# Four norms at stage borders, taken by token halves, in a two-block transformer kernel

## The chip, the cores and the metric

The kernel runs on one core of one Trainium2 chip. The metric is the device time of one execution, in microseconds; the number given for a kernel is the median of its runs. The core's engines are TensorE (PE, with its weight loads as PEld), VectorE (DVE), ScalarE (ACT), GpSimd (POOL) and SyncE (SP), which here issues the loads. They work side by side and meet at semaphores.

## What is computed

Two blocks of a network over 256 latent tokens of width 1024, in float32. The first block is an attention and recurrence layer and a neighbourhood attention layer. The second block carries 256 further context tokens beside the latent ones, so 512 in all. Its layers are feed-forward ("ffn"), a short convolution, and grouped-query attention. All of them have this frame:

```
mod = silu(c) @ mod_w[i] + mod_b[i]                       # shift, scale, gate; one set for latents, one for context
h   = rms(x) * g * (1 + scale) + shift                    # the norm in front of each layer
x   = x + 0.5 * gate * ((silu(h @ w1) * (h @ w3)) @ w2)    # feed-forward
x   = x + gate * ((b * dwconv3(c * v)) @ w_out)           # convolution: b, c, v = split(h @ w_in)
x   = x + gate * (attend(q, k, v) @ w_o)                  # attention; keys and values from latents and context
```

where `rms(x) = x / sqrt(mean(x*x) + 1e-6)` runs over the 1024 features of a token. A norm therefore needs every feature of a token, which is every output tile of the stage in front of it.

## The kernel before

Activations lie with features on the 128 partitions: `XT` is 128 x 8 x 512, eight k of 128 features, with the latent tokens in columns 0 to 255 and the context tokens in 256 to 511. The matmuls work in float32 by two parts: activation = `Hh` + `Hl`, weight = `Wh` + `Wl`, and `three` (line 1296) issues three matmuls for each product. Each weight tile of 128 x 2048 (128 x 1408 in the second half of a feed-forward) is loaded by SyncE into `raw`, copied by ScalarE into `Wh` (`split`, line 513), and the remainder `Wl` is made by VectorE (`split`, line 799). Two buffers each hold raw, Wh and Wl, so ScalarE's copy of tile n waits for TensorE to end tile n - 2 (`tile_done`), and TensorE's tile n waits for `lo_ready`.

The stages run in a fixed order (`STAGES`), each tile of 256 output features (`conv_in` 12 tiles, `conv_out` 4, `ffn*_up` 22). In `ffn*_down` an output of 128 features takes two tiles, one for each half of the contraction, 16 tiles in all. The sixth entry of a stage is `gemv`: so many rows of the modulation weights are dotted on VectorE with each tile (`modulation_of`, line 848; two `dot` instructions of 128 x 1024 for each row set, one for latents and one for context).

A stage that feeds a norm adds its output to `XT` (`residual` on VectorE, line 903, and `ffn_down`, line 938). ScalarE squares each finished k (`splits`, line 560), GpSimd adds the squares up in `tmp[:, 2]` (line 459), and TensorE sums over partitions by matmuls with ones into `psN` (`sum_of_sums`, then the last one or two k in `norm`). VectorE makes the mean, GpSimd the power -0.5, TensorE spreads it over partitions (`spread`, line 1350), and then VectorE (`scaled`), ScalarE (`Hh`) and VectorE (`Hl`) make the eight k of the next input; the first tile of the next stage waits for each k (`h_ready`). Every one of these steps takes all 512 tokens. The copies of the second weight tile of the next stage stand between the mean and the scaling:

```python
split(S[name].n0 + 1, early=True)
dve.wait_ge(n_spread, i + 1)
```

`SUMMED` says how many of GpSimd's additions are made (6 behind a feed-forward, 5 behind `conv_out`). The order of each engine is written out by hand at the end of its program (`norm`, `linear`, `ffn_down` in turn).

## Time and profile before

| | us |
|---|---|
| median of 3 runs | 2092.98 |
| lowest and highest | 2090.76, 2093.58 |
| the profiled execution | 2093.39 |
| its span on the core | 2091.6 |
| TensorE busy | 1908.9 (91%) |
| TensorE weight loads busy | 1624.7 (78%) |
| VectorE busy | 1402.9 (67%) |
| ScalarE busy | 683.9 (33%) |
| GpSimd busy | 126.5 (6%) |

The profile is one execution. A row of its timeline gives the start from the beginning of the span, the duration, the engine, the line of the kernel, what is written and read, and in brackets how long the engine was idle before and what released it. A matmul's duration overlaps the next; the distance of two starts is what one costs. PEclk is the granted clock of TensorE as a share of 2.4 GHz; its two levels are 1.00 (2.4 GHz) and 0.50 (1.2 GHz).

### The profile page before, as it was taken

The numbers are of one execution on the slowest core, as the hardware profiler recorded it, in microseconds if no ns is written. First come the engines' busy times: TensorE is split into PE (matmuls) and PEld (weight loads), VectorE is DVE, ScalarE is ACT, GpSimd is POOL, SyncE is SP. The second block draws the span as 40 slices with busy tenths as digits, with TensorE's granted clock in tenths as the row PEclk, the third lists the DMA queues.
The fourth block names the chain that finished last, engine by engine and source line by source line (L and its number), as shares of the span: only waits on it lengthen the run. The fifth ranks groups of instructions, "written<-read, shape, count | busy, mean of one in ns | idle before, by whom it ended". The sixth has DMA issues, their size and how long they took to land.

```text
span 2091.6 us, 26725 instructions
## 1 busy us (share of the span) xinstructions
PE 1908.9 (91%) x10092; PEld 1624.7 (78%) x10092; DVE 1402.9 (67%) x2091; ACT 683.9 (33%) x910; POOL 126.5 (6%) x78
## 2 busy tenths in 40 slices
PE   2973799789999998998999999989999998889998
PEld 2952788778888887886788888878888887678998
DVE  7868799986666676668766666676666225856554
ACT  2443356432222213332322222232222223444432
POOL 2001300200000010002000001100000010010000
PEclk9975799889999999999999999999999999999999
DMA  9840955423443443334333344434333323223444
GB/s 377 313 168 3 238 206 188 181 93 149 150 150 125 167 175 124 134 148 151 121 143 133 146 149 159 164 121 151 141 134 118 105 94 122 91 81 141 162 163 158
DMA packets 75737, 315.77 MB, mean 151 GB/s; under 512 B 19060, under 2 KB 22904, under 8 KB 56344
## 3 DMA queue, kind: packets, MB, share of 16 engines
q1 hardware_dynamic: 75136, 314.15, 41.9%
q8 instruction: 36, 0.59, 0.1%
q10 hardware_dynamic: 536, 0.79, 0.1%
q14 instruction: 29, 0.24, 0.0%
HBM read 313.86 MB, written 1.06 MB: 151 GB/s over the span
## 4 chain that ended last, share of the span: by engine, by line
PE 74%; DVE 18%; ACT 3%; issue 2%; DMA 1%; POOL 1%; SPq 0%; DVEq 0%; ACTq 0%
PE acc L1294 72%; DVE Wl L810 4%; ACT Wh L526 2%; DVE tmp L797 2%; PE psN L1294 1%; DVE psGT L842 1%; DVE psGT L839 1%; DVE psGT L845 1%; DVE najunk L845 1%; DVE najunk L842 1%; DVE XT L797 1%; DMA afirst<-in_ada_w 1%; DVE small L967 1%; PE psN L1356 1%; DVE tmp L985 1%
## 5 line engine op out<-in xcount | busy, mean ns | idle before, releaser
L1294 PE MATMUL acc<-Hh,Wh 128*128 128x512 f32 (+1 forms) x2320 | 809.0, 349 | 57.1 <-DVE Hl L797 23.4
L1294 PE MATMUL acc<-Hl,Wh 128*128 128x512 f32 (+1 forms) x2320 | 801.1, 345 | 0.0
L1294 PE MATMUL acc<-Hh,Wl 128*128 128x512 f32 (+1 forms) x2320 | 800.4, 345 | 0.0
L810 DVE TENSOR_TENSOR Wl<-raw,Wh 128x2048 fp32r<-128x2048 f32 (+1 forms) x214 | 449.6, 2101 | 273.0 <-ACT Wh L526 273.0
L1294 PEld LDWEIGHTS acc<-Hh,Wh 128*128 128x128 f32 x2320 | 448.5, 193 | 119.3 <-issue 62.2
L526 ACT ACTIVATE Wh<-raw 128x2048 fp32r<-128x2048 f32 (+1 forms) x214 | 374.3, 1749 | 352.0 <-PE acc L1294 336.7
L1294 PEld LDWEIGHTS acc<-Hl,Wh 128*128 128x128 f32 x2320 | 448.7, 193 | 50.6 <-issue 0.7
L1294 PEld LDWEIGHTS acc<-Hh,Wl 128*128 128x128 f32 x2320 | 448.1, 193 | 50.7
L1294 PE MATMUL acc<-hidh,Wh 128*128 128x512 f32 (+1 forms) x704 | 259.0, 368 | 0.9 <-DVE Wl L810 0.9
L1294 PE MATMUL acc<-hidl,Wh 128*128 128x512 f32 (+1 forms) x704 | 258.6, 367 | 0.0
L1294 PE MATMUL acc<-hidh,Wl 128*128 128x512 f32 (+1 forms) x704 | 258.6, 367 | 0.0
L797 DVE SCALAR_TENSOR_TENSOR tmp<-tmp,acc 128x512 f32<-128x512 f32 (+1 forms) x176 | 109.3, 621 | 130.0 <-ACT tmp L593 120.3
L593 ACT ACTIVATE tmp<-acc 128x512 f32<-128x512 f32 (+1 forms) x88 | 47.9, 544 | 453.2 <-PE acc L1294 453.2
L842 DVE SCALAR_TENSOR_TENSOR psGT<-graw,cb 128x1024 f32<-128x1024 f32 x122 | 169.3, 1388 | 0.4
L459 POOL TENSOR_TENSOR tmp<-tmp 128x512 f32<-128x512 f32 (+1 forms) x44 | 89.8, 2041 | 1313.7 <-ACT tmp L557 1156.4
L845 DVE SCALAR_TENSOR_TENSOR psGT<-graw,cb 128x1024 f32<-128x1024 f32 x122 | 154.0, 1262 | 4.2
L1294 PEld LDWEIGHTS acc<-hidh,Wh 128*128 128x128 f32 x704 | 132.6, 188 | 24.6 <-DVE Wl L810 1.1
L1294 PEld LDWEIGHTS acc<-hidh,Wl 128*128 128x128 f32 x704 | 132.6, 188 | 23.9
L1294 PEld LDWEIGHTS acc<-hidl,Wh 128*128 128x128 f32 x704 | 132.6, 188 | 23.8
L934 DVE TENSOR_TENSOR hidl<-tmp,hidh 128x512 f32 (+3 forms) x88 | 55.1, 626 | 71.5 <-ACT hidh L596 71.5
L797 DVE SCALAR_TENSOR_TENSOR XT<-acc,mod,XT 128x256 f32 (+3 forms) x88 | 36.0, 454 | 88.3 <-PE acc L1294 88.3
L596 ACT ACTIVATE hidh<-tmp 128x512 f32 (+3 forms) x88 | 50.9, 578 | 133.8 <-DVE tmp L797 133.8
(222 smaller groups left out, 1193.8 us busy)
## 6 DMA issues: line engine op xcount, KB each, us to landing
raw<-in_ffn_up SPq DMA_DIRECT2D x88, 1024.0 KB, 4.7
graw<-in_mod_w SPq DMA_DIRECT2D x144, 512.0 KB, 5.4
raw<-in_ffn_down SPq DMA_DIRECT2D x64, 704.0 KB, 4.0
graw<-in_ada_w SPq DMA_DIRECT2D x32, 512.0 KB, 6.2
raw<-in_odd_in SPq DMA_DIRECT2D x16, 1024.0 KB, 4.9
raw<-in_even_in SPq DMA_DIRECT2D x12, 1024.0 KB, 6.8
raw<-in_conv_in SPq DMA_DIRECT2D x12, 1024.0 KB, 4.7
afirst<-in_ada_w SPq DMA_DIRECT2D x8, 1024.0 KB, 13.1
```

Source lines behind the costliest of these rows:

```text
L459: nc.gpsimd.tensor_tensor(tmp[:, 2, 0:n], tmp[:, 0 if k == 1 else 2, 0:n], tmp[:, k % 2, 0:n], ALU.add).then_inc(n_sum, 1)
L526: nc.scalar.activation(Wh[:, half, 0:f], raw[:, slot, 0:f], ACT.Copy).then_inc(hi_ready, 1)
L593: nc.scalar.activation(tmp[:, b, 0:s.tokens], acc[b][0][:, 0:s.tokens], ACT.Tanh, scale=0.5)\
L596: nc.scalar.activation(at3(hidh, t, s.tokens), tmp[:, 3, 0:s.tokens], ACT.Copy).then_inc(ffn_hi, 1)
L797: return nc.vector.scalar_tensor_tensor(out=out, in0=a, scalar=s, in1=b, op0=op0, op1=op1)
L810: nc.vector.tensor_tensor(Wl[:, half, 0:f], raw[:, slot, 0:f], Wh[:, half, 0:f].bitcast(f32), ALU.subtract)\
L839: nc.vector.scalar_tensor_tensor(out=psGT[:, :], in0=graw[:, slot, :], scalar=0.5, in1=cfirst[:, :], op0=ALU.mult, op1=ALU.mult, accum_out ...
L842: nc.vector.scalar_tensor_tensor(out=junk[:, :], in0=graw[:, slot, :], scalar=0.5, in1=cb[:, 0, :], op0=ALU.mult, op1=ALU.mult, accum_out= ...
L845: nc.vector.scalar_tensor_tensor(out=junk[:, :], in0=graw[:, slot, :], scalar=0.5, in1=cb[:, 1, :], op0=ALU.mult, op1=ALU.mult, accum_out= ...
L934: nc.vector.tensor_tensor(at3(hidl, t, c), tmp[:, 3, c], at3(hidh, t, c).bitcast(f32), ALU.subtract)\
L967: link(nc.vector.tensor_reduce(out=out, in_=L[:, u % 2, :, :], op=ALU.max, axis=AX.X))
L1294: return nc.tensor.matmul(out, lhsT, rhs, start=start, stop=stop)
```

## The change

At the four norms in front of `conv_in`, `ffn1_up`, `ffn2_up` and `gqa_kv` (`HALVED`):

- The last output of the stage in front is made by token halves. In `ffn*_down` the last tile pair runs as latent half of the first weight buffer, sum of sums, context half of it, latent half of the second buffer, context half of it, with the latent norm's sums inside the last part. In `conv_out` the last tile runs as sum of sums, both outputs of the latents, both of the context.
- The latent half then has its own residual, square, sums, mean, power, spread and eight k, signalled by new semaphores (`lat_*`). The context residual stands behind the third latent k on VectorE, its squares there on ScalarE, and its sums and spread inside the first tile on TensorE, in another bank (`psT[1]`). The context's eight k follow.
- The copies `Wh` and `Wl` of the next stage's second tile stand between the latent k and the context k.
- The next stage's first two tiles run as tile 0 latents, tile 1 latents, tile 0 context, tile 1 context. In front of `gqa_kv` the order is key latents, value latents, key context, value context.
- `gemv` of `conv_out` goes from 2 to 1, that of `gqa_out` from 0 to 1; the rows dotted in the stages between are four earlier ones in turn.

```diff
-    ("conv_out", 4, 16, 0, TOK, 2, "dve"),
+    ("conv_out", 4, 16, 0, TOK, 1, "dve"),
...
-    ("gqa_out", 4, 16, 0, LAT, 0, "dve"),
+    ("gqa_out", 4, 16, 0, LAT, 1, "dve"),
...
+        if name in ("ffn0_down", "ffn1_down", "ffn2_down"):
+            drained[by] -= 1
...
+        HALVED = {n: i for i, n in enumerate(["conv_in", "ffn1_up", "ffn2_up", "gqa_kv"])}
+        LAST = {n: (KC - 2, KC - 1) if n == "ffn1_up" else (KC - 1,) for n in HALVED}
+        LAT_SQ0 = {n: sum(len(LAST[m]) for m in HALVED if HALVED[m] < HALVED[n]) for n in HALVED}
+        CL, CC = slice(0, LAT), slice(LAT, TOK)
+
+        def halved(s):
+            return X_TO.get(s.name) in HALVED
...
+                if name in HALVED:
+                    pool.wait_ge(lat_mean, HALVED[name] + 1)
+                    power(rstd[:, 0:2], means[:, 0:2], 2).then_inc(lat_rstd, 1)
+                    pool.wait_ge(n_mean, i + 1)
+                    power(rstd[:, 2:4], means[:, 2:4], 2).then_inc(n_rstd, 1)
+                    return
...
+                    if halved(s) and t == s.tiles - 1:
+                        if s.tiles < KC:
+                            act.wait_ge(drained["dve"], s.drained0 + t)
+                            square(name, 2 * t - 2)
+                            square(name, 2 * t - 1)
+                            next_split(s, t, t % PER, t // PER)
+                            act.wait_ge(lat_res, HALVED[name] + 1)
+                        else:
+                            next_split(s, t, t % PER, t // PER)
+                            act.wait_ge(lat_res, HALVED[name] + 1)
+                        for k in LAST[name]:
+                            if k == LAST[name][0]:
+                                act.wait_ge(n_sum, SUM0[name] + 5)
+                            square_half(name, k, CL)
+                        return
...
+                        act.wait_ge(lat_t, KC * HALVED[name] + k + 1)
+                        nc.scalar.activation(Hh[:, k, CL], tmp[:, k % 2, CL], ACT.Identity, bias=affine(name, k, 0)[1])\
+                            .then_inc(lat_hi, 1)
+                        if k == 2:
+                            act.wait_ge(drained["dve"], S[X_FROM[name]].drained1)
+                            for q in LAST[name]:
+                                square_half(name, q, CC)
+                    split(S[name].n0 + 1, early=True)
...
+                if ffn:
+                    split(S[name].n0)
+                dve.wait_ge(lat_done, l + 1)
+                residual_half(0, CL).then_inc(lat_res, 1)
+                meanwhile()
+                mean(0, psN, lat_ss, l + 1).then_inc(lat_mean, 1)
+                if not ffn:
+                    split(S[name].n0)
+                dve.wait_ge(lat_spread, l + 1)
+                scaled(0, 0, CL, psN).then_inc(lat_t, 1)
+                for k in range(KC):
+                    if k + 1 < KC:
+                        if k > 0:
+                            dve.wait_ge(lat_ready, KC * l + k)
+                        scaled(k + 1, 0, CL, psN).then_inc(lat_t, 1)
+                    dve.wait_ge(lat_hi, KC * l + k + 1)
+                    low(k, 0, CL).then_inc(lat_ready, 1)
+                    if k == 2:
+                        dve.wait_ge(tile_done, s.n0 + s.tiles)
+                        residual_half(1, CC).then_inc(drained["dve"], 1)
+                    if k == 6:
+                        mean(1, psT[1], n_ss, i + 1).then_inc(n_mean, 1)
+                split(S[name].n0 + 1, early=True)
+                dve.wait_ge(n_spread, i + 1)
+                scaled(0, 1, CC, psT[1]).then_inc(n_t, 1)
+                for k in range(KC):
+                    if k + 1 < KC:
+                        if k > 0:
+                            dve.wait_ge(h_ready, H0[name] + k)
+                        scaled(k + 1, 1, CC, psT[1]).then_inc(n_t, 1)
+                    dve.wait_ge(n_hi, KC * i + k + 1)
+                    low(k, 1, CC).then_inc(h_ready, 1)
...
+                pe.wait_ge(lo_ready, s.n0 + 1)
+                pe.wait_ge(drained[s.by], s.drained0)
+                part(0, CL, lat_ready, KC * l, {3: ctx_sums, 7: ctx_spread})
+                pe.wait_ge(lo_ready, s.n0 + 2)
+                pe.wait_ge(drained["dve"], prev.drained1)
+                part(1, CL, lat_ready, KC * l, {})
+                part(0, CC, h_ready, H0[name], {}).then_inc(tile_done, 1)
+                part(1, CC, h_ready, H0[name], {}).then_inc(tile_done, 1)
...
+                        sum_of_sums(X_TO[s.name])
+                        for h, hc in enumerate((CL, CC)):
+                            for j in range(2):
+                                for k in range(KC):
+                                    last = three(acc[u % 2][h][:, j * LAT:(j + 1) * LAT], u % 2, j * KC + k, xh[:, k, hc], xl[:, k, hc],
+                                                 k == 0, k == KC - 1)
+                                if h == 1 and j == 0:
+                                    lat_sums(X_TO[s.name])
+                            last.then_inc((lat_done, tile_done)[h], 1)
+                        lat_spreads(X_TO[s.name])
+                        return
...
+                    name, t = X_TO[s.name], s.tiles - 2
+                    pe.wait_ge(drained["dve"], s.drained0 + t - 2)
+
+                    def part(h, w, cols, beside=None):
+                        pe.wait_ge(lo_ready, s.n0 + t + w + 1)
+                        for k in range(W2H):
+                            kk = w * W2H + k
+                            last = three(acc[1][h][:, cols], w, k, hidh[:, kk, cols], hidl[:, kk, cols], kk == 0, kk == FC - 1)
+                            if beside and k == 4:
+                                beside(name)
+                        return last
+
+                    part(0, 0, CL)
+                    sum_of_sums(name)
+                    part(1, 0, CC).then_inc(tile_done, 1)
+                    part(0, 1, CL).then_inc(lat_done, 1)
+                    part(1, 1, CC, lat_sums).then_inc(tile_done, 1)
+                    lat_spreads(name)
...
+                    for h, bank in enumerate((psN, psT[1])):
+                        for b in range(2):
+                            nc.tensor.matmul(bank[:, b:b + 1], tmp[:, 2, (2 * h + b) * P:(2 * h + b + 1) * P], ones[:, 0:1],
+                                             start=b == 0, stop=False, skip_group_check=True)
+                    return
...
-            norm("gqa_kv")
...
+            keys(CL, lat_ready, KC * HALVED["gqa_kv"])
...
+                    keys(CC, h_ready, H0["gqa_kv"]).then_inc(tile_done, 1)
...
-                if tb == 1:
+                if tb == 2:
```

## Rows read from the trace of the kernel before

**Rows 1.** The page, chain that ended last: shares of the span by engine.

```profile
PE 74%; DVE 18%; ACT 3%; issue 2%; DMA 1%; POOL 1%; SPq 0%; DVEq 0%; ACTq 0%
```

**Rows 2.** Timeline, TensorE, border to conv_in. Columns: start us, us, what, [idle before].

```profile
776.41 0.40 PE L1294 MATMUL acc<-hidh,Wh 128*128 128x512 f32 x1
...
784.11 0.95 PE L1356 MATMUL psN<-ones,tmp 128*128 128x1 f32 x8
...
801.41 0.77 PE L1294 MATMUL acc<-Hh,Wh 128*128 128x512 f32 x1 [3.41 <-DVE Hl L797]
...
807.09 0.41 PE L1294 MATMUL acc<-Hl,Wh 128*128 128x512 f32 x1
```

**Rows 3.** Timeline, GpSimd and ScalarE, the same border.

```profile
778.65 2.21 POOL L459 TENSOR_TENSOR tmp<-tmp 128x512 f32<-128x512 f32 x1 [13.19 <-ACT tmp L557]
...
795.81 1.02 POOL L451 TENSOR_TENSOR rstd<-means,expo 128x4 f32<-128x4 f32 x1 [14.96 <-DVE means L875]
...
784.37 1.92 ACT L526 ACTIVATE Wh<-raw 128x2048 fp32r<-128x2048 f32 x1 [5.80 <-PE acc L1294]
...
815.25 0.60 ACT L542 ACTIVATE cv_proj<-acc 128x512 f32<-128x512 f32 x1 [3.64 <-PE acc L1294]
...
826.13 0.60 ACT L542 ACTIVATE cv_proj<-acc 128x512 f32<-128x512 f32 x1 [7.99 <-PE acc L1294]
```

**Rows 4.** Timeline, a norm over 256 tokens (ffn3_up): VectorE, then TensorE.

```profile
1884.35 0.47 DVE L797 SCALAR_TENSOR_TENSOR tmp<-XT,mod,psN 128x256 f32<-128x256 f32 x1
1885.40 0.49 DVE L797 SCALAR_TENSOR_TENSOR Hl<-tmp,mod,Hh 128x256 fp32r<-128x256 f32 x1 [0.18 <-ACT Hh L585]
...
1886.32 0.48 DVE L797 SCALAR_TENSOR_TENSOR Hl<-tmp,mod,Hh 128x256 fp32r<-128x256 f32 x1
...
1886.03 0.55 PE L1294 MATMUL acc<-Hh,Wh 128*128 128x256 f32 x1 [3.45 <-DVE Hl L797]
```

**Rows 5.** Chain that ended last, stretch of gqa_out: start us, us, what.

```profile
1855.54 23.04 PE acc L1294 x192
```

**Rows 6.** Timeline, end of conv_out: VectorE, GpSimd, TensorE.

```profile
974.55 0.48 DVE L797 SCALAR_TENSOR_TENSOR XT<-acc,mod,XT 128x256 f32<-128x256 f32 x1
...
976.94 4.83 POOL L459 TENSOR_TENSOR tmp<-tmp 128x512 f32<-128x512 f32 x2 [6.38 <-ACT tmp L557]
...
981.83 0.27 PE L1356 MATMUL psN<-ones,tmp 128*128 128x1 f32 x1 [0.17 <-POOL tmp L459]
...
997.11 0.77 PE L1294 MATMUL acc<-Hh,Wh 128*128 128x512 f32 x1 [2.93 <-DVE Hl L797]
```

**Rows 7.** Timeline, first tiles of ffn1_up: ScalarE, VectorE.

```profile
1010.41 0.60 ACT L593 ACTIVATE tmp<-acc 128x512 f32<-128x512 f32 x1 [3.10 <-PE acc L1294]
...
1014.96 2.29 DVE L810 TENSOR_TENSOR Wl<-raw,Wh 128x2048 fp32r<-128x2048 f32 x1 [1.11 <-ACT Wh L526]
```

**Rows 8.** Timeline, TensorE, end of ffn2_down and first query tile.

```profile
1729.09 0.50 PE L1356 MATMUL psN<-ones,tmp 128*128 128x1 f32 x4
...
1773.56 0.28 PE L1294 MATMUL acc<-Hh,Wh 128*128 128x256 f32 x1
```

**Rows 9.** Timeline, VectorE, odd_out, and the last residual of gqa_out.

```profile
398.27 0.48 DVE L797 SCALAR_TENSOR_TENSOR XT<-acc,ada,XT 128x256 f32<-128x256 f32 x1
...
401.25 2.33 DVE L842 SCALAR_TENSOR_TENSOR psGT<-graw,cb 128x1024 f32<-128x1024 f32 x1
...
405.99 0.48 DVE L797 SCALAR_TENSOR_TENSOR XT<-acc,ada,XT 128x256 f32<-128x256 f32 x1
...
1878.60 0.48 DVE L797 SCALAR_TENSOR_TENSOR XT<-acc,mod,XT 128x256 f32<-128x256 f32 x1 [1.46 <-PE acc L1294]
```

**Rows 10.** Timeline, TensorE; then windows: busy by engine, PEclk, DMA, GB/s.

```profile
96.14 0.36 PE L1294 MATMUL acc<-Hh,Wh 128*128 128x256 f32 x1 [2.86 <-DVE Wl L810]
...
96.00:102.00 6.00, 5.87 (x37) 5.90 (x38) 5.86 (x8) 0.00 (x0) 0.00 (x0) 0.72 0.86 305
...
1810.00:1814.00 4.00, 2.45 (x11) 1.41 (x12) 3.57 (x12) 2.74 (x7) 0.00 (x0) 1.00 0.00 0
```

More of the change, by code:

```diff
@@ L212, in build @@
         c_tanh = sem("c_tanh")
+        lat_done, lat_res, lat_sq, lat_ss, lat_mean, lat_rstd, lat_spread, lat_t, lat_hi, lat_ready = (
+            sem("lat_" + x) for x in ("done", "res", "sq", "ss", "mean", "rstd", "spread", "t", "hi", "ready"))
         nmx = small[:, 0:64]
@@ L905, in step @@
                 def step(t, u, i):
+                    if halved(s) and t == s.tiles - 1:
+                        modulation_of(s, t, u, i)
+                        return
                     next_split(s, t, u, i)
@@ L940, in step @@
                 def step(t, u, i):
+                    if halved(s) and isinstance(t, int) and t == s.tiles - 1:
+                        modulation_of(s, t, u, i)
+                        return
                     next_split(s, t, u, i)
@@ L1302, in three, with first_two_halved, part @@
                 return mm(out, wl, xh, False, last)
+            def first_two_halved(s):
+                name, prev = s.name, S[X_FROM[s.name]]
+                l = HALVED[name]
+                def part(t, c, ready, base, beside):
+                    n = s.n0 + t
+                    for k in range(KC):
+                        pe.wait_ge(ready, base + k + 1)
+                        for j in range(2):
+                            last = three(acc[t][j][:, c], n % SPLIT, j * KC + k, Hh[:, k, c], Hl[:, k, c], k == 0, k == KC - 1)
+                        if k in beside:
+                            beside[k](name)
+                    return last
[7 more added lines that the diff above has]
+                part(1, CC, h_ready, H0[name], {}).then_inc(tile_done, 1)
@@ L1320, in step @@
                     last.then_inc(tile_done, 1)
-                if begin:
+                if begin or halved(s):
                     for t in range(begin, s.tiles):
                         step(t, t % SPLIT, t // SPLIT)
+                elif s.name in HALVED:
+                    first_two_halved(s)
+                    tiles(pe, s, SPLIT, 0, lambda t, u, i: None if isinstance(t, int) and t < SPLIT else step(t, u, i), head=1)
                 else:
@@ L1342, in step, with last_halved @@
                     last.then_inc(tile_done, 1)
+                def last_halved():
+                    name, t = X_TO[s.name], s.tiles - 2
[7 more added lines that the diff above has]
+                                beside(name)
+                        return last
+                    part(0, 0, CL)
[4 more added lines that the diff above has]
+                    lat_spreads(name)
                 def but_last(t, u, i):
+                    if isinstance(t, int) and halved(s) and t >= s.tiles - 2:
+                        if t == s.tiles - 2:
+                            last_halved()
+                        return
                     if isinstance(t, int) and t == s.tiles - 1 and s.name in X_TO:
```

75 lines of the change are left out of this document (67 added, 8 removed).

## The prediction

> **What bounds the kernel now.** I read the chain that ended last first: TensorE holds 74% of it and VectorE 18% [rows 1]. The matmul stream sets the end, and everything else counts only where that stream stands still. So I went to the timeline of TensorE at the four borders. At the border to conv_in the last tile pair of ffn0_down begins at 776.41, the summing matmuls of the norm stand at 784.11, and one tile takes 784.11 - 776.41 = 7.70 us (33 matmuls, 0.233 each). The stream therefore ends at 784.11 + 0.81 + 7.70, about 792.7, and the next stage starts at 801.41 [rows 2]. Its first 13 steps take 807.09 - 801.41 = 5.68 us; at full pace (0.227, because a tile of 48 takes 826.13 - 815.25 = 10.88 us [rows 3]) they would take 2.95. The border thus costs 8.7 us of gap and 2.7 us at the lower clock level, 1.2 GHz. The borders to ffn2_up and gqa_kv have the same shape. The border behind conv_out is longer, 981.83 to 997.11 [rows 6], because VectorE, with four dot instructions a tile, reaches the last residual late. These four, some 50 us with the clock, are what the change works on.
>
> **Width.** Each 512-column matmul of the last pair and of the first two tiles becomes two of 256. 192 of 256 columns take 23.04 us, 0.120 each [rows 5]. That is 2 x 0.120 - 0.233 = 0.007 more for each of 66, and 0.240 - 0.227 = 0.013 more for each of 96: 1.7 us per border, on the path. The Trainium skill, "TensorE: Matmul & The Clock Gate", section "Back-to-back issue gap", puts the fixed part of a matmul at about 2.5 ns, by which the same split would cost 0.4 us per border; the rows show 13 ns, and the rows decide.
>
> **Border to conv_in, step by step** (us from 776.41). Latent half through buffer 0: 33 x 0.12 = 3.96. Now TensorE meets the sum of sums, which earlier stood one whole tile later (7.70) and found GpSimd done. GpSimd ends its add at 778.65 + 2.21 = 780.86 [rows 3], at 4.45: a new wait of 0.5. Sums (0.81): 5.3. Context half, buffer 0: 9.3. Latent half, buffer 1: 13.2. Meanwhile ScalarE's split of the next stage's first weights, released by buffer 0 at 9.3 (1.92 long [rows 3]), and VectorE's remainder (2.29 [rows 7]) end at 13.8; the residual of the latent half (0.5) and its square (0.4) end at 14.7. TensorE does 15 matmuls of the last context half until 15.0 and meets the sums without a wait; the mean and the GpSimd power (1.02 [rows 3], 1.3 with the handovers) are hidden by the 18 matmuls left (2.2); without that cover they would cost 1.3. Sums 0.5, matmuls 2.2, spreads 0.4: 18.1. From the first scaled half to the first matmul takes 1886.03 - 1884.35 = 1.68 [rows 4]: TensorE starts at about 20.0, where before it was 25.0. So far 5 us are gained.
>
> What follows gives most of it back. VectorE makes a k of 256 columns in 1886.32 - 1885.40 = 0.92 [rows 4], TensorE eats it in 6 x 0.12 = 0.72. Behind k = 2 VectorE must wait for the tile, do the context residual (0.48), and ScalarE must square it (0.4) ahead of the next Hh: 0.85 more. The eighth k is ready at 20.0 + 6.4 + 0.85 = 27.3. **The second weight tile comes late:** before, its split ran in the gap ahead of the norm; now both engines queue it behind all eight latent k. ScalarE 1.9 and VectorE 2.29 end at 30.8, TensorE has been done since 28.5 and stands 2.4 us. Queued behind that Wl on VectorE is the whole context norm, which is ready in time. Three halves remain, 3 x 48 x 0.12 = 17.3: 48.2. Before: 801.41 + 96 x 0.227 + 2.7 = 825.9, which is 49.5. Gain 1.3. Tile 2's weights (one copy, Wh, Wl behind tile 0: 5.5) just arrive within the 5.76 of tile 1's context half.
>
> **ffn2_up.** The same, but tile 2's weights wait behind ScalarE's tanh and Hh copy of tile 0: tanh at 1010.41, Wl done at 1014.96 + 2.29 = 1017.25 [rows 7], 7.0 us behind tile 0's end, 7.2 with the handover. Tile 1 covered it with 10.88 us; now only its context half of 5.76 stands there: 1.4 us lost. Sum +0.1.
>
> **conv_out to ffn1_up.** Here the sum of sums stands ahead of the whole last tile, and it needs the squares of k = 4 and 5, which come from tile 2, just ended. Tile 3 ended at about 981.4 (the 981.83 of the sums [rows 6] less their wait of 0.17 and the tail of a matmul) and began 48 x 0.233 = 11.2 earlier, at 970.2. Tile 2's residual starts then; before it was at 974.55, and GpSimd's two adds from it ended at 976.94 + 4.83 = 981.77 [rows 6], 7.2 us later. So the adds end at 977.6 and **TensorE stands 7.4 us ahead of tile 3**, where nothing else is queued for it. Before, tile 3 covered this all but those 0.17. The clock falls in it: one low stretch, 2.2 by the 11 slow steps at 997.11 (4.71 us against 2.49). The halved dots (four instructions taken out, about 10.6 us of VectorE) bring the residuals on time, but that is what the wait now begins from. From 970.2: 7.4 + sums 0.8 + latent 5.8 + context with sums 6.7 + low clock 2.2 + spreads 0.4 = 23.3; first matmul 25.1; two residuals and two squares in the chain, 1.65; second weights at 36.8; three halves 54.1; tile 2 late by 1.4: 55.5. Before: 997.11 + 21.8 + 2.2 = 1021.1, that is 50.9. Loss 4.6.
>
> **gqa_kv.** Second tile at 30.9; two value blocks 5.76, the context keys 5.76, a value block 2.88, key sums 1.7, the last 2.88: 49.9. Before the first query matmul was at 1773.56 [rows 8], 52.2 behind 1729.09 - 7.70 = 1721.4 [rows 8]. Gain 2.3, of which 0.6 goes again because the key mean now stands behind the dots of the next tile: -1.7. SyncE's rope and first query load wait for the context residual, some 4 us later than before; ScalarE wants them 20 us later, nothing lost.
>
> **gqa_out.** The dots taken from conv_out land here, one pair a tile. Their loads come two tiles ahead; the queue has room. Tiles take only 5.76 us [rows 5], VectorE then has residual 0.9, Wl 2.3, dots 2.6. odd_out shows such a stage: residuals at 398.27 and 405.99, 7.72 apart, one dot 2.33 long beside GpSimd's add instead of 1.23 [rows 9]. The Trainium skill, "GPSIMD Engine Reference", section "Key points", says that GpSimd shares its SBUF interfaces with VectorE and contends with instructions that have two SBUF inputs; this row agrees. The adds here have half the width, so I take 6.7 a step: residuals at 1868.8, 1875.5, 1882.2 against 1878.60 now [rows 9]: +3.6, straight on the path, since the norm waits for it. Bounds: no contention, +1.1; odd_out's rhythm, +6.1.
>
> **The clock.** The 2.4 us stand ahead of the second weights is new, once per border. The trace has an idle stretch of 2.86 us at full level; behind it 37 matmuls of 256 columns take 5.87 us where 37 x 0.12 = 4.44 would do, with the granted clock at a mean of 0.72 [rows 10]: a fall costs 1.4. Against it, 1810 to 1814 has TensorE busy for 2.45 of 4 us and stays at 1.00 [rows 10]. The stand lies between; I take a fall at two of four borders, 2.8, with 0 and 5.6 as bounds.
>
> **Sum:** -1.3 + 4.6 + 0.1 - 1.7 + 3.6 + 2.8 = +8.1. The profiled execution took 2093.4 (span 2091.6 and 1.8 around it), so 2101.5; the median of the three runs lies 0.4 below it, 2092.98, so **2101.1**.
>
> **Rivals.** (a) The small loss: the short stands leave the clock alone and the dots in gqa_out meet little of GpSimd. 5.3 - 2.5 = +2.8, 2095.8, a difference that can't be told from none. For it: the attention stage's clock. Chance 0.22. (b) The heavy loss: a fall at all four borders and odd_out's full rhythm, 5.3 + 5.6 + 2.5 = +13.4, 2106.4. For it: odd_out is the nearest stage. 0.18. (c) The other side, faster: the wait ahead of conv_out's last tile is not paid, because GpSimd's adds are done when tile 3 begins. Then 7.4 and the 2.2 of its low clock are off, 5.3 - 9.6 = -4.3, with the gqa_out bound of +1.1 -6.8: 2086.2. It decides for faster once that wait is under about 1 us with no falls. Against it: the adds can't begin before tile 2 has ended, and two take 4.8. With other gains unseen, 0.08. That the change doesn't do what it says (the latent half not starting early) would show as (b).
>
> **Chances.** Forecast 0.52, (b) 0.18, (a) 0.22, (c) 0.08. About 0.2% is what a measurement of this kernel can tell from none, 2088.8 to 2097.2: faster 0.08, same 0.22, slower 0.70. Range 2092.5 to 2107.5: it takes in (a) and (b) and the 0.7 us by which the adds may be shorter.
>
> **What would show it.** In the changed kernel: the gap at the conv_in border falls from 8.7 to about 2 us, and a new TensorE wait of about 2.4 us for Wl stands ahead of the second tile, four times; a TensorE wait of about 7.4 us for GpSimd's adds ahead of conv_out's last tile; 1.4 us for Wl ahead of tile 2 of ffn1_up and ffn2_up; the last residual of gqa_out about 3.6 us behind its matmuls. The prediction is wrong if the 7.4 us wait is missing, if the second weights are ready in time, or if the granted clock falls in the latent norm as well.

## The result, and the profile after

The changed kernel takes 2102.10 us, the median of 5 runs (2101.23 to 2104.47), against 2093.24 for the kernel before (2090.76 to 2093.68): 8.9 us more, a ratio of 1.0046 with a 95% interval of 1.0035 to 1.0057. The forecast was 2101.1, slower. The profiled execution took 2104.47 (span 2102.7), 11.1 more than the profiled one of before; the spans of its four other executions were 2099.4 to 2100.3.

The page of the changed kernel, the chain that ended last, beside [rows 1]: TensorE has gone from 74% to 77%, VectorE from 18% to 14%. VectorE lies less on the path, and the time is longer all the same.

```profile
PE 77%; DVE 14%; ACT 3%; issue 3%; POOL 1%; DMA 1%; SPq 0%; ACTq 0%; DVEq 0%; POOLq 0%
```

**The ledger.** I took ScalarE's copies of the weights (Wh<-raw, one for each of the 214 weight tiles, in the same order in every kernel) and subtracted the time of the same copy in the profile of before. Where this difference stays the same, nothing is won or lost; it moves at the borders, and in the attention stage. The table gives each stretch's share, us, for the changed kernel and for the experiments that follow ("early" is all up to conv_in's norm, which no kernel changes; half_width, which alters a whole stage, is told below).

| kernel | early | conv_in | conv_out | ffn2_up | gqa_kv | attention | gqa_out | ffn3_up |
|---|---|---|---|---|---|---|---|---|
| changed | +0.24 | -0.37 | +4.69 | +0.22 | -0.79 | +2.76 | +3.38 | +0.58 |
| sums_late | -2.02 | -0.35 | -3.45 | +0.18 | -0.80 | +2.85 | +3.38 | +0.57 |
| before_dots_moved | 0.00 | +0.04 | -3.99 | +0.26 | -0.93 | +1.21 | +3.38 | +0.03 |
| three_borders | -0.74 | -0.36 | -3.99 | +0.51 | -0.82 | +1.20 | +3.38 | -0.03 |
| three_dots_back | -1.60 | -0.36 | +0.02 | +0.19 | -0.79 | +2.79 | -0.01 | +0.54 |
| dots_back | -1.82 | -0.37 | +10.07 | +0.22 | -0.82 | +2.87 | 0.00 | +0.60 |
| drained_less | -0.37 | -0.39 | +5.03 | +1.26 | -2.29 | +2.81 | +3.38 | +0.58 |
| drained_narrow | -0.71 | -3.86 | +1.73 | -2.27 | -4.28 | +1.23 | +3.38 | +0.23 |
| moved_spread_dots | -0.01 | -0.67 | -5.46 | +0.08 | -0.93 | +1.24 | 0.00 | +0.83 |
| three_spread_dots | -1.34 | -0.39 | -3.99 | +0.44 | -0.81 | +1.20 | 0.00 | +0.82 |
| best4 | -1.34 | -0.38 | -3.11 | +1.22 | -0.99 | 0.00 | 0.00 | +1.33 |

The early stretch differs by up to 2 us between profiles of kernels that are the same there; so one profile's span is good to about 2 us. The changed kernel's +0.24 is the highest; that may be why its profile stands 2.2 above the difference of the medians, but its other four executions left no trace. The columns behind it repeat to 0.1 or so where the code is the same and the low stretches of TensorE's clock (times at 1.2 GHz) have the same length, and then they can be read finer than the medians. Where these stretches differ, columns of the same code differ too: the old norm at conv_in comes out at +0.04 in before_dots_moved and at -0.67 in moved_spread_dots, the one behind conv_out at -3.99 and -5.46.

**TensorE at the border to conv_in** (timeline; start us, us, what, [idle before]). The gap of [rows 2] is gone, and three short ones stand in its place: ahead of the sums, ahead of the first latent tile, ahead of the second weights.

```profile
776.65 0.28 PE L1409 MATMUL acc<-hidh,Wh 128*128 128x256 f32 x1
...
781.14 0.61 PE L1570 MATMUL psN<-ones,tmp 128*128 128x1 f32 x4 [0.43 <-POOL tmp L471]
...
796.39 0.36 PE L1409 MATMUL acc<-Hh,Wh 128*128 128x256 f32 x1 [1.73 <-DVE Hl L850]
...
806.91 0.39 PE L1409 MATMUL acc<-Hh,Wh 128*128 128x256 f32 x1 [1.89 <-DVE Wl L863]
```

**The same view at ffn2_up and gqa_kv.** The first latent tile of ffn2_up waits 3.90 for VectorE's residual, and then finds its second weights ready; gqa_kv goes as conv_in:

```profile
1355.48 0.61 PE L1570 MATMUL psN<-ones,tmp 128*128 128x1 f32 x4 [0.44 <-POOL tmp L471]
...
1372.91 0.55 PE L1409 MATMUL acc<-Hh,Wh 128*128 128x256 f32 x1 [3.90 <-DVE XT L850]
...
1745.86 0.36 PE L1409 MATMUL acc<-Hh,Wh 128*128 128x256 f32 x1 [1.73 <-DVE Hl L850]
...
1756.37 0.39 PE L1409 MATMUL acc<-Wh,Hh 128*128 128x256 f32 x1 [2.13 <-DVE Wl L863]
```

**The border behind conv_out**, the same view, answering to [rows 6, 7]. Here the sums of the earlier squares stand ahead of the whole last tile:

```profile
976.55 0.98 PE L1570 MATMUL psN<-ones,tmp 128*128 128x1 f32 x4 [6.30 <-POOL tmp L471]
...
997.38 0.55 PE L1409 MATMUL acc<-Hh,Wh 128*128 128x256 f32 x1 [4.29 <-DVE XT L850]
...
1025.47 0.47 PE L1409 MATMUL acc<-Hh,Wh 128*128 128x512 f32 x1 [1.36 <-DVE Wl L863]
```

GpSimd's two adds there, and one step of gqa_out on VectorE with its last residual, for [rows 9]. Weights, two dots and the residual follow each other without a wait, 6.6 us from one residual to the next (1875.48 to 1882.09), where TensorE takes 5.76 for the tile:

```profile
972.69 3.72 POOL L471 TENSOR_TENSOR tmp<-tmp 128x512 f32<-128x512 f32 x2 [5.91 <-ACT tmp L575]
...
1875.48 0.87 DVE L850 SCALAR_TENSOR_TENSOR XT<-acc,mod,XT 128x256 f32<-128x256 f32 x2
1876.27 2.28 DVE L863 TENSOR_TENSOR Wl<-raw,Wh 128x2048 fp32r<-128x2048 f32 x1
1878.47 1.77 DVE L895 SCALAR_TENSOR_TENSOR psGT<-graw,cb 128x1024 f32<-128x1024 f32 x1
...
1880.33 1.59 DVE L898 SCALAR_TENSOR_TENSOR psGT<-graw,cb 128x1024 f32<-128x1024 f32 x1
...
1882.09 0.87 DVE L850 SCALAR_TENSOR_TENSOR XT<-acc,mod,XT 128x256 f32<-128x256 f32 x2
...
1888.66 0.87 DVE L850 SCALAR_TENSOR_TENSOR XT<-acc,mod,XT 128x256 f32<-128x256 f32 x2
```

**The clock** (table by stretch: us, busy us and instructions of PE, PEld, DVE, ACT, POOL, then the granted clock, DMA share, GB/s). The rows are, in turn: the latent norm at conv_in and the stretch behind its second weights, conv_out's last tile, the latent norms of ffn1_up and ffn2_up, and two stretches of the attention stage, which [rows 10] show at full level before. gqa_kv goes as conv_in (0.60 from 1746 to 1750). So the level is low in the latent norm at each of the four borders.

```profile
797.00:801.00 4.00, 3.89 (x20) 3.43 (x20) 3.40 (x9) 2.03 (x5) 0.00 (x0) 0.61 0.01 4
808.00:812.00 4.00, 4.00 (x24) 4.00 (x23) 3.82 (x10) 2.12 (x5) 0.00 (x0) 0.57 0.84 337
975.00:983.00 8.00, 6.45 (x33) 6.48 (x34) 1.39 (x3) 0.00 (x0) 1.41 (x1) 0.57 0.00 0
995.00:1003.00 8.00, 5.62 (x28) 5.65 (x28) 5.75 (x14) 4.72 (x9) 0.00 (x0) 0.57 0.34 137
1372.00:1378.00 6.00, 5.09 (x24) 5.12 (x25) 4.32 (x11) 3.68 (x7) 0.00 (x0) 0.50 0.00 0
1814.00:1818.00 4.00, 2.67 (x7) 1.53 (x8) 2.52 (x8) 2.23 (x5) 0.00 (x0) 0.63 0.00 0
1859.00:1863.00 4.00, 4.00 (x16) 3.50 (x15) 1.31 (x3) 1.35 (x1) 0.00 (x0) 0.57 0.00 0
```

So 8.1 of the 10.7 us that the ledger finds between the profiles are conv_out's border (4.69) and gqa_out (3.38), 2.8 are the clock in the attention, and three of the four borders are within 1 us of nothing. Even the 0.37 gained at conv_in can't be put to the halves, since moved_spread_dots has -0.67 there with the old norm.

### The profile page after: what moved, and what is told of

Same layout as the page of the kernel before. It is cut to its first block, busy times and chain, and to the rows that moved or that the text cites. A ratio compares the mean times of both kernels' runs of the same rounds, so it can differ in the third digit from the quotient of the medians.

```text
span 2102.7 us, 27881 instructions
## 1 busy us (share of the span) xinstructions
PE 1922.5 (91%) x10674; PEld 1661.2 (79%) x10674; DVE 1408.3 (67%) x2099; ACT 688.1 (33%) x915; POOL 130.6 (6%) x82
## 4 chain that ended last, share of the span: by engine, by line
PE 77%; DVE 14%; ACT 3%; issue 3%; POOL 1%; DMA 1%; SPq 0%; ACTq 0%; DVEq 0%; POOLq 0%
PE acc L1409 73%; DVE Wl L863 3%; ACT Wh L544 2%; DVE tmp L850 2%; PE psN L1409 1%; DVE psGT L892 1%; DMA afirst<-in_ada_w 1%; DVE psGT L895 1%; DVE Hl L850 1%; DVE XT L850 1%; DVE psGT L898 1%; POOL rstd L463 1%; POOL tmp L471 0%; PE psGT L1409 0%; PE psN L1561 0%
## 5 line engine op out<-in xcount | busy, mean ns | idle before, releaser
L1409 PE MATMUL acc<-Hh,Wh 128*128 128x256 f32 (+1 forms) x2432 | 830.0, 341 | 58.2 <-DVE Hl L1107 20.7
L1409 PE MATMUL acc<-Hl,Wh 128*128 128x256 f32 (+1 forms) x2432 | 820.4, 337 | 0.0
L1409 PE MATMUL acc<-Hh,Wl 128*128 128x256 f32 (+1 forms) x2432 | 819.6, 337 | 0.0
L1409 PEld LDWEIGHTS acc<-Hh,Wh 128*128 128x128 f32 x2432 | 471.5, 194 | 117.8 <-issue 62.3
L1409 PEld LDWEIGHTS acc<-Hl,Wh 128*128 128x128 f32 x2432 | 472.2, 194 | 45.7 <-issue 0.7
L1409 PEld LDWEIGHTS acc<-Hh,Wl 128*128 128x128 f32 x2432 | 471.5, 194 | 45.3
L1409 PE MATMUL acc<-hidh,Wh 128*128 128x512 f32 (+1 forms) x770 | 269.8, 350 | 0.9 <-DVE Wl L863 0.9
L1409 PEld LDWEIGHTS acc<-hidh,Wh 128*128 128x128 f32 x770 | 144.8, 188 | 22.2 <-DVE Wl L863 1.1
L1409 PEld LDWEIGHTS acc<-hidl,Wh 128*128 128x128 f32 x770 | 144.8, 188 | 21.1
L1409 PEld LDWEIGHTS acc<-hidh,Wl 128*128 128x128 f32 x770 | 144.8, 188 | 21.0
```

What stands on the lines that cost most here:

```text
L1409: return nc.tensor.matmul(out, lhsT, rhs, start=start, stop=stop)
```

## The experiments

Every time below is a median, beside that of the kernel before in the same series (2092.8 in the first, 2092.2 in the second, 2092.41 in the third), and I compare the distances to it. The changed kernel stands at +8.9.

**sums_late.** Is the wait ahead of conv_out's last tile the loss there?

```diff
-                        sum_of_sums(X_TO[s.name])
                         for h, hc in enumerate((CL, CC)):
...
                             last.then_inc((lat_done, tile_done)[h], 1)
+                            if h == 0:
+                                sum_of_sums(X_TO[s.name])
```

> The changed kernel, but ahead of conv_out's last tile TensorE no longer waits for GpSimd's adds: it takes the latent half first and the matmuls of the sum of sums behind it. Theory (that wait is the loss at this border): TensorE stood 6.30 us, and of the 15.6 us from 977.0 to the spread at 992.66 some 2.8 were lost at the low clock. The latent half now fills 970.0 to 975.8, the adds end at about 976.3, a wait of 0.5 stays, the context half ends near 984.9: everything behind comes 7.4 earlier, 2102.1 - 7.4 = 2094.7. Rival (the wait only moves on: the latent residual and its squares queue behind other work and the latent sums come late, or the clock falls again): under 3 us of gain, 2099 or more. Second rival (this border's loss is the second weights): no gain, 2102.

Measured: 2094.70, +1.9; ratio to before 1.0010 (1.0001 to 1.0019). In the ledger conv_out's border goes from +4.69 to -3.45, 8.1 less, and no other column behind "early" moves by more than 0.1. The trace shows 0.59 left of the wait of 6.30:

```profile
974.27 0.60 PE L1571 MATMUL psN<-ones,tmp 128*128 128x1 f32 x4 [0.59 <-POOL tmp L471]
...
978.11 0.95 PE L1446 MATMUL psN<-ones,tmp 128*128 128x1 f32 x8
...
986.87 0.55 PE L1409 MATMUL acc<-Hh,Wh 128*128 128x256 f32 x1 [4.29 <-DVE XT L850]
```

The theory holds: one call in the wrong place costs most of what the change loses, 7.0 of 8.9 by the medians and 8.1 in the ledger. The second rival falls, because all that stands behind this point (the 4.29, the second weights, tile 2) is as it was and comes along.

**before_dots_moved.** What do the dots do by themselves?

```diff
-    ("conv_out", 4, 16, 0, TOK, 2, "dve"),
+    ("conv_out", 4, 16, 0, TOK, 1, "dve"),
...
-    ("gqa_out", 4, 16, 0, LAT, 0, "dve"),
+    ("gqa_out", 4, 16, 0, LAT, 1, "dve"),
```

> The kernel before, with only the dots moved: conv_out one pair a tile instead of two, gqa_out one instead of none. Theory: gqa_out with the border behind it costs 4.0 more, as the two traces differ from 6.68 to 10.65 there; in conv_out VectorE's residual of tile 2 comes when the tile is done instead of 4.35 late, and so the border behind it is 4.35 shorter. Together -0.4, 2092.9. Rival (conv_out's border is not set by VectorE's lateness): only the 4.0 are left, 2097.2. Second rival (the dots in gqa_out are not the cause there, the loss comes from the halved norms or the clock): conv_out's gain alone, 2088.9.

Measured: 2092.22, -0.6 (0.9987 to 1.0005). conv_out's border is 3.99 shorter and gqa_out 3.38 longer: the move is worth nothing, since it pays at one place what it gains at another. That 3.38 is the same to 0.01 in all six kernels with one pair in gqa_out, whichever form the norms have.

**three_dots_back** and **three_borders.** What do the halves bring where no wait of GpSimd's stands in the way? Both take the border behind conv_out back to the old norm; the first also puts the dots back.

```diff
-        HALVED = {n: i for i, n in enumerate(["conv_in", "ffn1_up", "ffn2_up", "gqa_kv"])}
+        HALVED = {n: i for i, n in enumerate(["conv_in", "ffn2_up", "gqa_kv"])}
...
             linear(S["conv_out"], xh=cyh, xl=cyl)
+            norm("ffn1_up")
```

> The changed kernel with the norm behind conv_out in its old form and the dots where they were (conv_out two pairs, gqa_out none): only the three borders to conv_in, ffn2_up and gqa_kv go by halves. Theory: the ledger of the two traces gives -0.40, +0.22 and -0.80 for them, sum -1.0: 2092.3. Rival (the small sum is the traces' chance and the halves gain what they were meant to once alone): 2088 or less. Second rival (the new short low clock stretches weigh more over many executions): 2095 or more.

> The changed kernel with the norm behind conv_out in its old form, the dots as in the changed kernel (one pair in conv_out, one in gqa_out). Theory: three borders -1.0, gqa_out +4.0, and conv_out's border, now without VectorE's lateness, -4.35: 2093.24 - 1.3 = 2091.9. Against the changed kernel that is 10.2 less, the price of the halved form behind conv_out once the dots are moved. Rival (the old form's border is not shortened by moving the dots): 2096.2.

Measured: 2095.07, +2.3 (1.0003 to 1.0022), and 2092.70, -0.1 (0.9991 to 1.0009). The first is a miss by nearly 3 us, at the number of the second rival, and the ledger says where: the three borders are -0.36, +0.19 and -0.79 as in the changed kernel, but the attention stage costs 2.79, and I had left the attention out as a chance of one profile. It isn't: 2.8 came back in four more kernels with halves, and 1.2 even in before_dots_moved, whose code is that of before up to the attention's end but for the dots in conv_out and the rows dotted behind it. The second kernel is within 0.8 of what was expected. Against the changed kernel it is 9.0 less: the halved form behind conv_out, as it was made, costs that once the dots are moved.

**moved_spread_dots.** Is gqa_out's loss VectorE's volume between the residuals? On the kernel before with the dots moved; the lines that change:

```diff
                         take(a, u // 2 - 1)
+                if a is gqa:
+                    modulation_of(S["gqa_out"], 0, 0, 0, gjunk)
                 take(a, a.groups - 1)
...
                     next_split(s, t, u, i)
-                    modulation_of(s, t, u, i)
+                    if s.name != "gqa_out":
+                        modulation_of(s, t, u, i)
+                    elif t in (0, 2):
+                        m = t // 2 + 1
+                        modulation_of(s, m, m, 0)
...
             norm("ffn3_up", lambda: mod_scale(1, 2))
+            modulation_of(S["gqa_out"], 3, 3, 0)
```

> The kernel before with the dots moved (conv_out one pair a tile, gqa_out one), and in gqa_out the four pairs put where VectorE stands: the first ahead of the last part of the attention (it idles 4.45 us there in the trace of the changed kernel), the second ahead of tile 0's residual, the third ahead of tile 2's, the fourth behind the norm of ffn3_up. Theory (gqa_out's 3.4 us are VectorE's volume between residuals, 6.6 a tile against TensorE's 5.76): the last residual comes on time, 3.4 less than with one pair a tile; the fourth pair, 3.3 us behind the norm, gives back 0 to 1.5. 2092.2 - 2.6 = 2089.6, ratio to before 0.9985. Rival (what costs is that the dots slow GpSimd's adds, wherever they stand): 2091 to 2092. Second rival (the pair behind the norm holds up the weights of ffn3_up's tile 2 in full): 2092.

Measured: 2088.74, -3.5; ratio 0.9984 (0.9975 to 0.9993). It beats both kernels. In the ledger gqa_out goes from 3.38 to 0.00, and ffn3_up gives 0.8 back, 2.6 in all. This profile also has shorter low stretches at conv_in and behind conv_out (-0.67 and -5.46, where before_dots_moved has +0.04 and -3.99 with the same code), so not all of the 3.5 need come from the dots. The dots are no shorter beside GpSimd (1.77 and 1.59 below; the pairs that stand where GpSimd is idle take 1.23), but now VectorE has a wait ahead of the last residual, and [rows 9] have the same:

```profile
1865.55 1.77 DVE L842 SCALAR_TENSOR_TENSOR psGT<-graw,cb 128x1024 f32<-128x1024 f32 x1
...
1867.41 1.59 DVE L845 SCALAR_TENSOR_TENSOR psGT<-graw,cb 128x1024 f32<-128x1024 f32 x1
...
1872.85 0.88 DVE L797 SCALAR_TENSOR_TENSOR XT<-acc,mod,XT 128x256 f32<-128x256 f32 x2 [0.61 <-PE acc L1301]
```

The pair behind the norm costs 0.8 (ffn3_up +0.83): TensorE waits 1.34 for the weights of tile 2 instead of 0.40.

**drained_less** and **drained_narrow.** What sets the start of the second tile behind the latent norm? In both the wait ahead of the first latent tile is for one residual less; the second also makes VectorE's remainder of the second weights for 128 of 2048 columns.

```diff
-                pe.wait_ge(drained[s.by], s.drained0)
+                pe.wait_ge(drained[s.by], s.drained0 - (1 if s.by == "dve" else 0))
...
-                split(S[name].n0 + 1, early=True)
+                n1 = S[name].n0 + 1
+                dve.wait_ge(hi_ready, n1 + 1)
+                nc.vector.tensor_tensor(Wl[:, n1 % SPLIT, 0:P], raw[:, n1 % RAW, 0:P], Wh[:, n1 % SPLIT, 0:P].bitcast(f32), ALU.subtract)\
+                    .then_inc(lo_ready, 1)
                 dve.wait_ge(n_spread, i + 1)
```

> The changed kernel, but ahead of the first latent tile of ffn1_up and ffn2_up TensorE waits for one residual less: not for the context residual of the last output, which lies in the other accumulator. Theory (TensorE stood 4.29 and 3.90 us there instead of 1.7, but then had the second weights ready; VectorE's work from the spread to the second Wl, 8 k of 0.92, a residual and a Wl of 2.3, sets when the second tile starts): the first matmul comes 2.2 earlier twice and the gain is eaten by a new stand of about 2 us ahead of the second tile: 2101.9, 0.2 less. Rival (the wait was on the path in full): 4.5 less, 2097.6. Second rival (two stands instead of one let the clock fall twice): 2103.

> The kernel of the last run, and VectorE's remainder of the second weight tile at the four borders is made for 128 of its 2048 columns only (left out: 15/16 of the low part of that one tile's weights; the rest of the computation stands). It measures what the second Wl, behind the eight latent k, costs. Theory: 2.2 us of VectorE less ahead of the second tile. conv_in and gqa_kv stood 1.89 and 2.13 us for it: both gain about 1.9, and 1.7 each if the low clock stretch behind that stand goes as well; ffn1_up and ffn2_up gain 2.0 each, now that their first tile starts in time. Sum 7.8 without the clock, 11 with it: 2094.3 to 2091. Rival (TensorE stands for the k, 0.92 against 0.72, and the context norm follows as late as before): under 3 us, 2099 or more.

Measured: 2101.49, +9.3, no difference from the changed kernel's +8.9; and 2089.16, -3.0 (0.9982 to 1.0000), which is 12.3 less; its eleven executions lie in two groups, seven from 2087.7 to 2089.7 and four from 2092.5 to 2093.7. The first is as expected: at ffn2_up the first matmul comes 2.2 us sooner after the spread, and a stand of 2.36 for Wl has appeared, with 0.78 for the k. (At ffn1_up the first matmul comes sooner too, but no stand for Wl follows: the granted clock has a mean of 0.53 from 995 to 1006, and TensorE is slow enough to meet the weights.)

```profile
1370.43 0.36 PE L1409 MATMUL acc<-Hh,Wh 128*128 128x256 f32 x1 [1.73 <-DVE Hl L850]
...
1373.93 0.39 PE L1409 MATMUL acc<-Hh,Wh 128*128 128x256 f32 x1 [0.78 <-DVE Hl L850]
...
1380.94 0.57 PE L1409 MATMUL acc<-Hh,Wh 128*128 128x256 f32 x1 [2.36 <-DVE Wl L863]
```

ffn2_up even lost 1.0 (+0.22 to +1.26): the low stretch has moved from the latent half, where TensorE kept pace with VectorE anyway, to behind the second stand, where it counts. The latent half (first row) is now at full level, the tile behind the stand (second row) is not:

```profile
1371.00:1379.00 8.00, 6.80 (x52) 6.04 (x50) 5.93 (x15) 4.89 (x8) 0.70 (x1) 1.00 0.01 2
1381.00:1385.00 4.00, 4.00 (x21) 4.00 (x22) 3.71 (x9) 2.21 (x5) 0.00 (x0) 0.58 0.70 245
```

Without the second Wl the borders gain 3.5, 3.3, 3.5 and 2.0 against drained_less, more than the 7.8 to 11 in all that I expected. About 2.0 of each is the instruction (at conv_in the second tile begins 8.5 us behind the first instead of 10.5); at conv_in and ffn2_up the rest is the clock, which now doesn't fall there at all (the row below, conv_in's border); at gqa_kv it had not fallen in drained_less either, and the gain is the bare 2.0.

```profile
795.00:811.00 16.00, 14.41 (x112) 13.68 (x113) 13.33 (x32) 9.21 (x17) 0.69 (x1) 1.00 0.29 101
```

So VectorE's work from the spread to the second weights is what a halved norm costs, and the drained wait was no cost of its own. Part of that stretch is ScalarE's, which copies the second weights behind its own latent k: in the changed kernel VectorE stands 1.32 us for this copy. No run took it away.

```profile
804.56 2.29 DVE L863 TENSOR_TENSOR Wl<-raw,Wh 128x2048 fp32r<-128x2048 f32 x1 [1.32 <-ACT Wh L544]
```

**half_width.** The price of halving the columns, measured by itself: in the kernel before, ffn1_up takes its 512 columns as two halves.

```diff
+                    if s.name == "ffn1_up":
+                        for hc in (slice(0, LAT), slice(LAT, TOK)):
+                            for k in range(KC):
+                                ...
+                                for j in range(2):
+                                    last = three(acc[u % 2][j][:, hc], u % 2, j * KC + k, xh[:, k, hc], xl[:, k, hc], k == 0, k == KC - 1)
```

> The kernel before, with all matmuls of 512 columns in ffn1_up taken as two of 256 (22 tiles of 96 instead of 48 matmuls). It measures the price of the width alone. By the rows (0.120 for 256 columns, 0.2267 for 512) a tile takes 11.52 instead of 10.88 us: 22 x 0.64 = 14.1 more, 2106.9. The Trainium skill, TensorE: Matmul & The Clock Gate, section Back-to-back issue gap, has a fixed part of about 2.5 ns a matmul, which would give 22 x 48 x 0.0025 = 2.6 more, 2095.4. Rival: twice as many instructions are also held up by their issue, more than 14.

Measured: 2111.65 (2 runs), +19.4. From the second tile on the copies fall back by 0.64 us a tile, 13.4 in 21 tiles, the forecast rate to two digits; the other 4.7 are the first tile, whose context half now runs in full behind the norm's last k instead of beside it, which I hadn't counted (TensorE waits 0.72 for each of the last two k in the latent half). 0.64 us over 48 matmuls are 13 ns for each extra one. A stretch of one tile's length in the middle of the stage has TensorE busy throughout, at full clock, with 98 matmuls in it (96 of a tile and those cut at its ends), so that neither a wait nor the clock is in this price. The total lies where the rival put it, above 14, but the excess is in the first tile, not in the issue of the matmuls, so the rival falls:

```profile
1100.00:1111.52 11.52, 11.52 (x98) 11.52 (x97) 7.01 (x10) 3.03 (x3) 0.00 (x0) 1.00 0.36 137
```

**three_spread_dots** and **best4.** Do the repairs add up? The first is three_borders with the dots spread as above, the second the changed kernel with sums_late, drained_less and the spread dots.

> The changed kernel with the norm behind conv_out in its old form (three borders by halves), and gqa_out's four pairs of dots spread as in the run that did so on the kernel before. Theory: that run's 2088.74, and the three halved borders bring -1.0 by the ledger of the traces, while by the medians of 2092.7 and 2092.22 they bring +0.5; so 2087.7 to 2089.2, no difference from the old form at all four that can be told. Rival (the halves gain once VectorE is not late anywhere): 2086 or less. Second rival (they cost, by their two short stands and the clock in the attention behind them): 2090.5 or more.

> The changed kernel with all three repairs: the sum of sums behind the latent half of conv_out's last tile, the shorter wait ahead of ffn1_up and ffn2_up, the spread dots in gqa_out. Theory: 2102.1 - 7.4 - 0.6 - 3.4 = 2090.7: the losses stand in separate places and add up. Rival (the shorter wait costs once conv_out's wait is gone, since its border then has two stands, and the low clock twice): 2092.5 or more. Second rival (they are one loss, passed on from border to border): under 7 of the 11.4, 2095 or more.

Measured: 2089.76, -2.65 (0.9979 to 0.9997), and 2091.24, -1.2 (0.9986 to 1.0004). The first is 0.6 above the upper end of what was expected, the second 0.5 above its sum; as distances to before, -1.2 where the sum of the repairs gives -2.5. The losses stand in separate places and add up to within about 1 us. This is the sum of the medians alone: in best4's profile the attention's 2.8 are gone as well, which no repair was aimed at. All four norms by halves, mended, are 10.1 better than the change as it was made and 2.3 behind the old norms with the same spread dots.

**dots_back.** Was the move of the dots needed for the halved border?

> The changed kernel with only the dots where they were: conv_out two pairs a tile, gqa_out none; all four norms by halves. Theory: gqa_out gives its 4.0 back, but tile 2's residual in conv_out comes 4.35 late again, GpSimd's adds with it, and TensorE stands 10.7 instead of 6.3 us ahead of the last tile: 2102.1 - 4.0 + 4.4 = 2102.5. Rival (VectorE's lateness is hidden behind the halved last tile): 2098. Second rival (the longer stand costs a second low stretch): 2104.5.

Measured: 2103.33, +10.9 (1.0041 to 1.0068). The wait is there in the expected size:

```profile
978.65 0.98 PE L1570 MATMUL psN<-ones,tmp 128*128 128x1 f32 x4 [10.43 <-POOL tmp L471]
```

conv_out's border loses 10.07 instead of 4.69, 5.4 more, of which 4.1 is the wait and the rest not taken apart; gqa_out gives back its 3.38. The moved dots helped the change by 2.0.

## Why the prediction was right

Step by step, with the numbers of the ledger against the terms of the sum.

- **conv_out, the 7.4 us wait: right**, and the largest term. Measured 6.30 in its place; the two adds took 3.72, and 4.83 before [rows 6]. The border's end was given as 55.5 behind the start of the last tile and came at 1025.47 - 970.0 = 55.5; the loss of 4.6 is 4.69. This exactness is partly luck: the wait was 1.1 shorter than said, and the low clock behind it cost some 2.6 for 2.2 (sums 1.70 long, then 18 matmuls in 3.98 that take 2.16 at full level). And the first latent matmul came 2.3 later than I said (27.4 against 25.1), because I read the wait ahead of it wrongly: with `s.by` "dve" it counts the context residual of the last output too, which VectorE does behind k = 2. The second weights I had as late were then in time. The second tile began 36.6 behind the start, against 36.8 said, because VectorE's work up to the second weights sets it either way; at ffn2_up drained_less shows the one wait take the place of the other.
- **conv_in: right** in its steps (waits of 0.43 and 1.89 against 0.5 and 2.4; first matmul 19.7 behind the start against 20.0). The sum is -0.37 with a fall of the clock in it, against +0.1 (-1.3, and 1.4 for a fall).
- **ffn2_up: the sum right, a step wrong.** +0.22 against +0.1. The first latent matmul came 21.9 behind the start (1372.91 against 1350.99), not 20.0, by the same misread wait as at ffn1_up, and there was no stand for the second weights. Tile 2's weights came 1.45 late, against 1.4.
- **gqa_kv: -0.79 where -1.7 was said.** But before_dots_moved and moved_spread_dots, with the old norm there, also come out at -0.93. So the halves as they ran gained nothing at this border: their fall of the clock took 1.5 of it (drained_less, with the same code there and no fall, has -2.29), and the old form's own low stretch can be shorter with the same code. Over the 11 us that hold it the mean granted clock is 0.53 in before (1742 to 1753) and 0.69 in before_dots_moved, first row. At conv_in the old form shows the same, 0.54 in before (797 to 808) and 0.69 in moved_spread_dots, second row:

```profile
1738.00:1749.00 11.00, 6.95 (x25) 5.52 (x26) 10.67 (x23) 4.83 (x11) 0.13 (x1) 0.69 0.70 289
797.00:808.00 11.00, 7.13 (x27) 5.67 (x28) 10.67 (x23) 5.13 (x12) 0.00 (x0) 0.69 0.37 143
```

- **gqa_out: right.** The residuals were put 6.7 apart and came 6.6 apart; the last one 3.6 late, measured 3.4 (1888.66 against 1878.60 + 6.68). The dot beside GpSimd's add took 1.77 where it takes 1.23 alone, between the two bounds. With the border behind it 3.96. The Trainium skill, "GPSIMD Engine Reference", section "Key points", on which that step leaned for contention, agrees with these rows; the 2.33 a dot of odd_out's row was not reached, and the 6.7 taken below its 7.72 came within 0.1.
- **The clock, +2.8: right at the borders, and a stretch missing.** Behind the stands for the second weights it fell at two of the four borders, as I said, conv_in and gqa_kv. The row of 808 to 812 has a mean of 0.57 over 4 us of full work, so a fall costs 4 x 0.43 = 1.7, 3.4 for both against 2.8. Both are inside the columns of these borders. What I had put at nothing is the attention stage, 2.76, whose code is the same, and which I had taken as the evidence that such stretches stay at full level [rows 10]. With it the ledger behind "early" comes to 10.5 where the sum said 8.1. That the median came to 8.9, only 1.0 us from the forecast 2101.1, is luck: the medians lie 2.2 closer together than the profiles, and no run shows why.
- **Width, 1.7 a border: right.** half_width gives the 13 ns a matmul that the term used. The Trainium skill, "TensorE: Matmul & The Clock Gate", section "Back-to-back issue gap", gives the fixed part of about 2.5 ns for an isolated matmul and says that in a stream of weight loads and matmuls both set the spacing, so I had carried it to a case it does not cover. By it, an estimate, the 21 tiles would have cost 2.5 us; they cost 13.4.
- **The signs of being wrong that I named.** The 7.4 us wait was there. But the second weights were in time at two borders (ffn1_up and ffn2_up), where I had said a stand of 2.4 would come four times, and the granted clock fell in the latent norm at all four. By these signs the mechanism was right at conv_in, gqa_kv and conv_out's last tile, and only in part behind it. At ffn2_up, where both came, the column is +0.22, so there they cost next to nothing.

Of the rivals, (a) and (b) lie 6.3 below and 4.3 above the measured time; the clock did fall, and odd_out's full rhythm did not come. (c) named the right lever: taken away in sums_late, the wait and its low clock gave 8.1 (said: 9.6). This did not take the changed kernel below before, because the attention's clock and gqa_out remained. What makes the clock fall in the attention stage stays open. It isn't the halves alone, since before_dots_moved and half_width have one stretch there with the old norms (1.2 us), and best4 has none with the new. Nor is it the time of arrival alone: best4 and before_dots_moved enter the stage 4.65 and 4.62 us ahead of before, and one has a stretch and the other none. No run varied one thing in that stage.

## What to carry to other kernels

A gap that is filled by work from its own tail only moves the question to which engine must now deliver first: here each half's gain went into the 12 us that VectorE takes from the first scaled half to the end of the second weights (794.71 to 806.85 at conv_in), so count the other engine's whole volume up to the point where the stream runs free, not the first instruction's start. When the order of a stream is changed, go through every small call that stays at its old place and ask what its wait was hidden by; the sum of sums lost its cover at one border of four and cost 7 to 8 us, and moving this one call mends it. And spread side work into places where the engine waits for something else, one piece in each: that was worth 2.6 to 3.5 us here, about what the change was meant to bring at conv_in and gqa_kv together (3.0).

## What the runs showed of the hardware

- TensorE's clock in a stage with little to do hangs on more than that stage. The attention stage was at 2.4 GHz throughout in two kernels (before and best4), had one low stretch in six (1.2 us lost each) and two in five (2.8), with nearly the same instructions and waits in it: a price of 0 to 2.8 us for one stage whose code no edit touched, but for one pair of dots that three of the kernels put at its end.
- A low stretch cost nothing that the ledger shows while TensorE kept pace with VectorE (0.50 from 1372 to 1378 in the changed kernel, ffn2_up +0.22), and about 1.7 us where the stream ran free; so removing one idle time can cost by moving the next stretch (ffn2_up in drained_less, +1.0).
- Two matmuls of 256 columns instead of one of 512, weights loaded for each, cost 13 ns more, over 21 tiles of 48 pairs; hence 0.64 us a tile.
- VectorE's dot over 1024 columns from SBUF and a GpSimd add over 256 lengthen each other in gqa_out: the dots from 1.23 to 1.77 and 1.59, and two adds from 3.41 (before) to 3.91 (changed). The two dots shown above end 1.1 us behind the ends of the adds that they began beside (1880.24 behind 1879.14, 1881.92 behind 1880.83), little less than a dot takes alone, as if each had first waited for the add.
